# Prompt attention: the 128 x 128 turns of a block stand one by one between TensorE's other matmuls

## The chip, the cores and the metric

The kernel runs on one core of one Trainium2 chip. The metric is the time of one execution on the device in microseconds (us), as the median of three. A core has five engines that run side by side: TensorE (PE; its matrix unit shows as PE and its weight loads as PEld), ScalarE (ACT), VectorE (DVE), GpSimd (POOL) and SyncE (SP), which issues most of the transfers.

## The reference

One inference step of a two-layer encoder: 2048 prompt frames and 128 sample frames of width 1024. A gated short convolution comes first, then keys and values, then stick-breaking attention with 16 heads of 64, each layer with its norms and output projection. The change lies in the attention over the prompt:

```
z = q @ k.T * scale
log_keep = where(kpos < qpos, log_sigmoid(-z), 0)
after    = reverse cumulative sum of log_keep over the keys, without the key itself
a        = where(kpos < qpos, exp(log_sigmoid(z) + after), 0)
o        = a @ v
```

## The kernel before

**Tiling.** `phase_attend` goes through 8 pairs of heads, so 16 heads. A head has 10 units, each of 512 queries by 512 keys; 4 of them lie on the diagonal. A unit has 4 pieces (128 queries by up to 512 keys) and 4 blocks (128 keys by up to 512 queries). In all there are 640 pieces and 640 blocks.

**A piece.** TensorE scores it with two matmuls (L1806, L1807: the high and the low part of the keys against the same stationary queries). ScalarE takes two sigmoids of the score (L1882, L1883), VectorE runs the scan (L1933, L1939), GpSimd multiplies (L1989). The weights `a` now stand with queries on the partitions.

**A block.** The product with `v` needs keys on the partitions, so TensorE turns the block: `turn` (L1824 to L1834) issues one transposing matmul of 128 x 128 for each of its query tiles (L1832). That is four, or 4 - j for block j of a unit on the diagonal: 2176 turns in all. In a turn the stationary operand is the tile of `a` and the identity streams through. The turns of a block write one slot of `a_pt` (TS = 3 slots), and the last of them gives the semaphore `t_ready`. ScalarE copies the slot to `a_ath` (L1892, "high"), VectorE subtracts to get `a_atl` (L1949, "low"), and TensorE multiplies both with the values (L1819, L1821, "product").

**Chunks.** Between these TensorE also makes the projections of later heads' queries and of the gates: 280 chunks of six matmuls, 448 or 416 columns wide (L1850 to L1852).

**The order.** Every engine works through a list that `Line.draw_up` writes when the kernel is built. It plays the phase through with costs for each item (`work`, L1409 to L1439: the time that the engine is held, and the further time until the result is seen by others), and takes at each step the item that can start first, by `RANK` where several can. TensorE's list has the items score, turn, product and chunk. A turn costs `TURN * w / P` there, with 0.2 us more until it is seen (L1424). Chunks are let in by `spent`, the share of the planned time that is behind (L1457 to L1462). On the chip each engine then keeps its list's order and waits on semaphores.

Of the kernel before, what the change touches and what calls it, by code (L numbers as in the profile page):

```python
# [13 lines left out]
P = 128  # L14
# [15 lines left out]
QG = 4  # L30
# [1217 lines left out]

ENGINES = "PE", "ACT", "DVE", "POOL", "SP"
N_HEAD, N_OUT = 2 * NPAIR, 2 * NPAIR * NGQ  # L1250
TURN = 0.068
SCORE_LEAD, CHUNKS_END, CHUNKS_FROM, CHUNK_PACE = 13, 0.96, -0.01, 6


# [26 lines left out]
class Line:  # L1281


    def __init__(self):
        self.at = {}
        self.free = dict.fromkeys(ENGINES, 0.0)
        self.lines = {e: [] for e in ENGINES}
        self.loads = []
        self.pieces = [(h, n) for h in range(N_HEAD) for n in range(N_PIECE)]
        self.blocks = [(h, b) for h in range(N_HEAD) for b in range(N_BLOCK)]  # L1290
        self.outs = [(h, b) for h, b in self.blocks if ends_group(b)]
        self.chunks = all_chunks()
        self.gates = [c for c in self.chunks if c[3] == PARTS - 1]
        self.splits = [(un, m, half) for un in range(N_UN) for m in (Q, Z) for half in range(2) if (un, m) != (0, Q)]
        self.splits.sort(key=lambda s: (s[0], s[1]))
        self.next = collections.Counter()
        self.whole = sum(2 * pe_time(piece_width(n)) for _, n in self.pieces)
        self.whole += sum((QG - block_from(b) // P) * TURN + 2 * pe_time(QG * P - block_from(b))
                          for _, b in self.blocks)
        self.spent = 0.0  # L1300
        for part in range(PARTS):
            self.at["x", 0, 0, part] = X_LANDS[part]
        for half in range(2):
            self.at["split", 0, Q, half] = 0.0
        for h in range(2):
            for what in KEYS:
                self.at[what, h] = 0.0 if h == 0 else FIRST_DONE
            self.at["v_in", h] = V_LANDS if h == 0 else FIRST_DONE
        for m in (Q, Z):
            self.at["raw", 0, m] = 0.0  # L1310
        self.free["SP"], self.moved = X_LANDS[0] + 10.0, FIRST_DONE
# [97 lines left out]
    def work(self, what):  # L1409

        k = self.next[what]
        if what in ("score", "sigmoid", "scan", "weigh"):
            w = piece_width(self.pieces[k][1])
            if what == "score":
                return 2 * pe_time(w), 0.249 + 0.000469 * w - pe_time(w)
            if what == "sigmoid":
                return 2 * act_time(w), 0.185 - 0.000036 * w
            if what == "scan":
                return 0.06 + 0.0022 * w - (0.04 if w == P * QG and is_diagonal(PIECES[self.pieces[k][1]][0]) else 0), 0.135
            return pool_time(w), 0.09  # L1420
        if what in ("turn", "high", "low", "product"):
            w = QG * P - block_from(self.blocks[k][1])
            if what == "turn":
                return TURN * w / P, 0.2  # L1424
            if what == "high":
                return act_time(w), 0.185 - 0.000036 * w
            if what == "low":
                return dve_time(w), 0.15
            return 2 * pe_time(w), 0.249 + 0.000469 * w - pe_time(w)
        if what == "out":  # L1430
            return act_time(QG * P), 0.17
        if what == "values":
            return 1.12 + 2.4, 0.1
        if what == "split":
            return 1.21 + 0.69 + 1.24, 0.1
        w = PGROUPS[(self.chunks[k] if what == "chunk" else self.gates[k])[1]][1]
        if what == "chunk":
            return 3 * PART_KT * pe_time(w), 0.249 + 0.000469 * w - pe_time(w)
        return (act_time(w), 0.17) if what == "open" else (dve_time(w), 0.15)  # L1439
# [5 lines left out]
    def place(self, engine, what, start):  # L1445
# [12 lines left out]
        self.free[engine] = end = start + took  # L1458
        at = self.at
        line = self.lines[engine]  # L1460
        if engine == "PE" and what != "chunk":
            self.spent += took  # L1462
        end += seen
# [132 lines left out]
def phase_attend(nc, x_d, qz_v, w_room, qh_t, ql_t, kh_t, kl_t, sz_t, v_prompt, ident, oa_t, ob_t,  # L1596
# [4 lines left out]
    with ExitStack() as ctx:  # L1601
# [186 lines left out]
        def _(pe):  # L1788
            pe.sem_inc(t_ready, N_BLOCK)
            pe.sem_inc(av_done, N_BLOCK)  # L1790

            def score(pr, hh, n):
                u, q = PIECES[n]
                g, kp = UNITS[u]
                i, p0, w = QG * g + q, kp * Z_W, piece_width(n)
                if is_pair(pr, 0) and hh == 0:
                    if n == 0:
                        pe.wait_ge(early.first_loaded, 96)
                    elif g == ORDER[1] and is_diagonal(u) and q == 0:
                        pe.wait_ge(q_rest, 32)  # L1800
                elif n == 0:
                    pe.wait_ge(qk_loaded[hh], 96 * (pr + hh))
                pe.wait_ge(z_used, piece(pr, hh, n - ZS) + 1 + ZS)
                o = pz[:, n % ZS, 0:w]
                lhs = q2[hh][:, i * P:(i + 1) * P]
                pe.matmul(o, lhs, kh2[hh][:, p0:p0 + w], start=True, stop=False)  # L1806
                pe.matmul(o, lhs, kl2[hh][:, p0:p0 + w], start=False, stop=True).then_inc(z_ready, 1)  # L1807

            def multiply(pr, hh, b):
                u, j = BLOCKS[b]  # L1810
                c0, kb = block_from(b), QG * UNITS[u][1] + j
                first, last = is_diagonal(u) and j == 0, ends_group(b)
                if first:
                    wait_past(pe, o_read, (2 * pr + hh) * NGQ + ORDER.index(UNITS[u][0]))
                if b == 0:
                    pe.wait_ge(v_ready[hh], pr + 1)
                pe.wait_ge(at_split, blk(pr, hh, b) + 1)
                o = po[:, c0:QG * P]
                pe.matmul(o, v2[hh][:, kb, :, :], ath[:, b % AS, c0:], start=first, stop=False,  # L1819
                          skip_group_check=True)  # L1820
                pe.matmul(o, v2[hh][:, kb, :, :], atl[:, b % AS, c0:], start=False, stop=last,  # L1821
                          skip_group_check=True).then_inc(av_done, 1)

            def turn(pr, hh, b):  # L1824
                u, j = BLOCKS[b]
                if is_pair(pr, 0) and (hh, b) == (0, 0):
                    pe.wait_ge(ident_set, 1)
                if j == 0:
                    pe.wait_ge(weighted, piece(pr, hh, QG * u + QG) + N_PIECE)
                wait_past(pe, at_split, blk(pr, hh, b) + 1 - TS)  # L1830
                for q in range(block_from(b) // P, QG):
                    mm = pe.transpose(pt[:, turn_slot(pr, hh, b), q * P:(q + 1) * P].bitcast(F32R),  # L1832
                                      a_bits[:, unit_slot(hh, u), q, j * P:(j + 1) * P], ident_r[:, :])
                mm.then_inc(t_ready, 1)  # L1834

            def chunk(pr, gx, m, part):
                n = PGROUPS[gx][1]
                if part == 0:
                    if m == Z and makes_queries(pr, Q):
                        pe.wait_ge(q_low, NGX * pr + gx + 1)  # L1840
                    else:
                        wait_past(pe, z_gated, gate_number(pr, m, gx))
                if m == Q:
                    pe.wait_ge(x_loaded[part], 16 * (NGX * pr + gx + 1))
                if gx == 0 and part % (PARTS // 2) == 0:
                    pe.wait_ge(w_ready[m], 2 * pr + 1 + part // (PARTS // 2))
                for k in range(PART_KT):
                    kt = part * PART_KT + k
                    x_h, x_l = x[:, part, k, 0, 0:n], x[:, part, k, 1, 0:n]
                    pe.matmul(pq[:, 0:n], wh[m][:, kt, :], x_h, start=(kt == 0), stop=False)  # L1850
                    pe.matmul(pq[:, 0:n], wh[m][:, kt, :], x_l, start=False, stop=False)
                    mm = pe.matmul(pq[:, 0:n], wl[m][:, kt, :], x_h, start=False, stop=(kt == KT - 1))  # L1852
                if part == PARTS - 1:
                    mm.then_inc(pq_ready[m], 1)
                elif m == Z:
                    mm.then_inc(x_used[part], 1)

            def do(what, pr, hh, n):
                if what == "score":
                    score(pr, hh, n)  # L1860
                elif what == "turn":
                    turn(pr, hh, n)
                elif what == "product":
                    multiply(pr, hh, n)
                elif what == "chunk":
# [1 line left out]

            for item in lines["PE"]:
                do(*item)

        @block.scalar
        def _(act):
# [812 lines left out]
```

## Time and profile before

| | us |
|---|---|
| median of three runs (lowest, highest) | 2830.48 (2828.51, 2833.29) |
| the profiled execution | 2826.52 |
| its span, first to last instruction | 2824.9 |
| TensorE busy in it | 2767.3 |
| turns (L1832): 2176, first and last start | 1458.5, 2530.3 |

Times in the rows are us from the span's start. PE rows tell when a matmul starts and how long it is in the unit. Matmuls are pipelined, so what one costs is read from the starts of two that follow each other, not from its length. Several of one line in a row are merged ("x4"). A line of the program is written L1832. The granted clock is a share of 2.4 GHz.

### The profile page before, as it was taken

The page shows a single profiled execution, that of the slowest core. Times are in us where ns is not written, and L with a number is a line of the kernel's source. Part 1 is how long each engine was busy: PE and PEld are TensorE (multiplying, and loading weights), DVE is VectorE, ACT ScalarE, POOL GpSimd, SP SyncE. Part 2 cuts the span into 40 slices and gives each one's busy share as a digit, 9 for nine tenths or more (in the row PEclk, how much of TensorE's full clock was granted, in tenths as well). Part 3 has the DMA queues.
Part 4 walks back from the last instruction along what each step waited for, and adds up shares of the span by engine and source line. Part 5 has one row for each costly group of instructions (what it writes and reads, how often), then busy time and mean ns, then how long its engine had stood idle before and what let it go on. Part 6 is the DMA issues. An engine that isn't in the chain of part 4 may idle for free. (4 is left out here: it accounts for less than half of the span.)

```text
span 2824.9 us, 42046 instructions
## 1 busy us (share of the span) xinstructions
PE 2767.3 (98%) x14856; PEld 2420.5 (86%) x14856; DVE 1642.8 (58%) x2152; ACT 1316.6 (47%) x2733; POOL 1157.2 (41%) x1023
## 2 busy tenths in 40 slices
PE   7999999999999999999989999999999999989998
PEld 6999999999988888889978888888888888868886
DVE  5321232123244450102249999999999999998775
ACT  6000000000033341111148888888888888875443
POOL 3333333333220020002356877777777768651110
PEclk9999999999999999999999999999999999999999
DMA  5101110111064444424578676777777876767773
GB/s 159 39 25 37 38 38 22 38 38 38 9 210 134 126 155 151 173 102 153 166 216 267 197 244 198 236 215 216 221 223 208 251 203 208 220 187 210 231 225 105
DMA packets 280359, 433.33 MB, mean 153 GB/s; under 512 B 52578, under 2 KB 218594, under 8 KB 274180
## 3 DMA queue, kind: packets, MB, share of 16 engines
q1 hardware_dynamic: 269156, 391.41, 45.5%
q0 software_dynamic: 11040, 39.86, 4.8%
q8 instruction: 89, 1.46, 0.2%
q14 instruction: 74, 0.61, 0.1%
HBM read 307.40 MB, written 123.81 MB: 153 GB/s over the span
## 5 line engine op out<-in xcount | busy, mean ns | idle before, releaser
L1989 POOL TENSOR_TENSOR a_a<-a_a,a_prod 128x512 f32<-128x512 f32 (+3 forms) x640 | 661.9, 1052 | 272.0 <-DVE a_prod L1939 196.6
L1939 DVE TENSOR_TENSOR_SCAN a_prod<-a_keep,a_prod,a_restart 128x513 f32<-128x513 f32 x384 | 478.2, 1269 | 8.3 <-ACT a_keep L1883 7.5
L1882 ACT ACTIVATE a_a<-a_pz 128x512 f32<-128x512 f32 (+3 forms) x640 | 357.2, 559 | 70.9 <-PE a_pz L1807 46.6
L1949 DVE TENSOR_TENSOR a_atl<-a_pt,a_ath 128x512 fp32r<-128x512 f32 (+3 forms) x640 | 363.1, 599 | 32.3 <-ACT a_ath L1892 29.0
L1883 ACT ACTIVATE a_keep<-a_pz 128x512 f32<-128x512 f32 (+3 forms) x640 | 361.1, 565 | 0.0
L1892 ACT ACTIVATE a_ath<-a_pt 128x512 fp32r<-128x512 f32 (+3 forms) x640 | 332.8, 558 | 57.5 <-PE a_po L1821 34.1
L1832 PEld LDWEIGHTS a_pt<-a_ident,a_bits 128*128 128x128 f32 x2176 | 232.2, 141 | 51.7 <-DVE a_atl L1949 8.1
L279 POOL TENSOR_TENSOR w_wh<-w_raw,w_gain 128x1024 fp32r<-128x1024 f32 x22 | 42.6, 1936 | 534.6 <-PE v_pg L349 279.9
L1806 PE MATMUL a_pz<-a_kh,a_q 128*128 128x512 f32 (+3 forms) x640 | 247.6, 390 | 8.4 <-ACT a_keep L1883 5.8
L1819 PE MATMUL a_po<-a_ath,a_v 128*128 128x512 f32 (+3 forms) x640 | 250.1, 395 | 2.3 <-POOL a_v L2000 1.5
L1832 PE MATMUL a_pt<-a_ident,a_bits 128*128 128x128 f32 x2176 | 244.8, 242 | 7.1 <-DVE a_atl L1949 4.7
L1807 PE MATMUL a_pz<-a_kl,a_q 128*128 128x512 f32 (+3 forms) x640 | 234.0, 368 | 0.0
L347 PE MATMUL c_pg<-a_xh,w_wh 128*128 128x384 f32 (+1 forms) x640 | 231.1, 361 | 0.1
L347 PE MATMUL c_pg<-a_xh,c_wh 128*128 128x384 f32 (+1 forms) x640 | 230.7, 360 | 0.3 <-ACT c_cgate L496 0.3
L348 PE MATMUL c_pg<-a_xl,c_wh 128*128 128x384 f32 (+1 forms) x640 | 230.5, 360 | 0.0
L349 PE MATMUL c_pg<-a_xh,c_wl 128*128 128x384 f32 (+1 forms) x640 | 230.4, 360 | 0.0
L348 PE MATMUL c_pg<-a_xl,w_wh 128*128 128x384 f32 (+1 forms) x640 | 230.3, 360 | 0.0
L1821 PE MATMUL a_po<-a_atl,a_v 128*128 128x512 f32 (+3 forms) x640 | 229.1, 367 | 0.0
L349 PE MATMUL c_pg<-a_xh,w_wl 128*128 128x384 f32 (+1 forms) x640 | 228.8, 357 | 0.0
L531 DVE TENSOR_TENSOR c_u<-c_pg,c_cgate 128x512 f32<-128x512 f32 (+2 forms) x40 | 23.4, 586 | 317.9 <-PE c_pg L349 317.9
L1933 DVE TENSOR_TENSOR_SCAN a_prod<-a_keep,a_restart 128x128 f32<-128x128 f32 (+3 forms) x256 | 197.2, 805 | 8.7 <-ACT a_keep L1883 7.8
L500 ACT ACTIVATE c_sz<-c_pg 128x384 f32<-128x384 f32 (+1 forms) x40 | 21.4, 536 | 355.8 <-PE c_pg L349 355.8
(234 smaller groups left out, 6151.5 us busy)
## 6 DMA issues: line engine op xcount, KB each, us to landing
a_x<-x_d SPq DMA_DIRECT2D x84, 896.0 KB, 6.7
a_x<-x_d SPq DMA_DIRECT2D x56, 832.0 KB, 6.0
a_kh<-kh_t SPq DMA_DIRECT2D x32, 512.0 KB, 7.1
a_kl<-kl_t SPq DMA_DIRECT2D x32, 512.0 KB, 9.1
w_raw<-in_a_w_in POOLq DMA_DIRECT2D x30, 512.0 KB, 4.9
x<-f_xn POOLq DMA_DIRECT2D x17, 512.0 KB, 6.4
g_y_in<-sz_t SPq DMA_DIRECT2D x17, 512.0 KB, 7.6
g_x<-x SPq DMA_DIRECT2D x17, 512.0 KB, 4.1
```

The lines of the kernel that those rows point to most:

```text
L347: pe.matmul(out, w_h[:, kt, :], x_h[:, kt, r], start=(kt == 0), stop=False)
L348: pe.matmul(out, w_h[:, kt, :], x_l[:, kt, r], start=False, stop=False)
L349: mm = pe.matmul(out, w_l[:, kt, :], x_h[:, kt, r], start=False, stop=(kt == KT - 1))
L1806: pe.matmul(o, lhs, kh2[hh][:, p0:p0 + w], start=True, stop=False)
L1819: pe.matmul(o, v2[hh][:, kb, :, :], ath[:, b % AS, c0:], start=first, stop=False, skip_group_check=True)
L1832: mm = pe.transpose(pt[:, turn_slot(pr, hh, b), q * P:(q + 1) * P].bitcast(F32R), a_bits[:, unit_slot(hh, u), q, j * P:(j + 1) * P], ident ...
L1882: act.activation(a[:, s, q, 0:w], pz[:, n % ZS, 0:w], ACT.Sigmoid, scale=SCALE)
L1883: act.activation(keep[:, n % KS, 0:w], pz[:, n % ZS, 0:w], ACT.Sigmoid, scale=-SCALE).then_inc(z_used, 1)
L1892: act.activation(ath[:, b % AS, c0:], pt[:, turn_slot(pr, hh, b), c0:], ACT.Copy).then_inc(at_hi, 1)
L1939: dve.tensor_tensor_scan(prod[:, s, 0:w + 1][:, ::-1], keep[:, n % KS, 0:w + 1][:, ::-1], restart[:, 0:1].broadcast_to([P, w + 1]), prod[: ...
L1949: dve.tensor_tensor(atl[:, b % AS, c0:], pt[:, turn_slot(pr, hh, b), c0:], ath[:, b % AS, c0:].bitcast(F32), ALU.subtract).then_inc(at_spl ...
L1989: pool.tensor_tensor(part, part, prod[:, n % PS, after:after + w], ALU.mult).then_inc(weighted, 1)
```

## The change

Each block's turns go into a queue, `turns_left`. `turn` issues the first of them at once. After each following matmul of a score, a product or a chunk, `between` issues one more. `turn_rest` issues what is left before the next block's first turn, at a "rest" mark, and at the end of the list. The planner has a turn cost 0.0595 us in place of 0.068, has a block seen 0.21 us later for each turn past the first, and puts a "rest" mark ahead of an item that starts, in the plan, after the block's turns are to be seen.

```
-TURN = 0.068
+TURN, TURN_APART = 0.0595, 0.21
...
             if what == "turn":
-                return TURN * w / P, 0.2
+                return TURN * w / P, 0.2 + TURN_APART * (w // P - 1)
...
+        if engine == "PE":
+            if what != "turn" and start > self.turn_seen:
+                line.append(("rest", 0, 0, 0))
+            elif what == "turn":
+                self.turn_seen = end + seen
...
                 pe.matmul(o, lhs, kh2[hh][:, p0:p0 + w], start=True, stop=False)
+                between()
                 pe.matmul(o, lhs, kl2[hh][:, p0:p0 + w], start=False, stop=True).then_inc(z_ready, 1)
+                between()
...
-                for q in range(block_from(b) // P, QG):
-                    mm = pe.transpose(pt[:, turn_slot(pr, hh, b), q * P:(q + 1) * P].bitcast(F32R),
-                                      a_bits[:, unit_slot(hh, u), q, j * P:(j + 1) * P], ident_r[:, :])
-                mm.then_inc(t_ready, 1)
+                turns_left.extend((pr, hh, b, q) for q in range(block_from(b) // P, QG))
+                turn_one()
+
+            def turn_one():
+                pr, hh, b, q = turns_left.popleft()
+                u, j = BLOCKS[b]
+                mm = pe.transpose(pt[:, turn_slot(pr, hh, b), q * P:(q + 1) * P].bitcast(F32R),
+                                  a_bits[:, unit_slot(hh, u), q, j * P:(j + 1) * P], ident_r[:, :])
+                if q == QG - 1:
+                    mm.then_inc(t_ready, 1)
+
+            def turn_rest():
+                while turns_left:
+                    turn_one()
+
+            def between():
+                if turns_left:
+                    turn_one()
...
                 elif what == "turn":
+                    turn_rest()
                     turn(pr, hh, n)
+                elif what == "rest":
+                    turn_rest()
...
             for item in lines["PE"]:
                 do(*item)
+            turn_rest()
```

The products' two matmuls and the chunks' six have `between` after each of them in the same way.

## Rows read from the trace of the kernel before

**Rows 1.** The page: each engine's busy time, its share and its instructions.
```profile
PE 2767.3 (98%) x14856; PEld 2420.5 (86%) x14856; DVE 1642.8 (58%) x2152; ACT 1316.6 (47%) x2733; POOL 1157.2 (41%) x1023
```
**Rows 2.** Stretches of the span: window, length, busy time (instructions) by engine, clock, DMA.
```profile
core 0: us, PE busy (x) PEld busy (x) DVE busy (x) ACT busy (x) POOL busy (x), PEclk, DMA share, GB/s
1458.00:1560.00 102.00, 95.31 (x560) 81.75 (x560) 88.60 (x114) 80.49 (x177) 67.43 (x63) 1.00 0.87 251
1560.00:2440.00 880.00, 876.79 (x5323) 775.11 (x5322) 841.96 (x1112) 760.76 (x1691) 659.67 (x626) 1.00 0.74 220
2440.00:2535.00 95.00, 85.75 (x523) 73.57 (x522) 87.19 (x121) 77.92 (x176) 55.35 (x55) 0.96 0.62 187
```
**Rows 3.** TensorE in order of time around four turns in a row (start, duration).
```profile
1799.81 0.39 PE L1807 MATMUL a_pz<-a_kl,a_q 128*128 128x512 f32 x1
1800.04 0.46 PE L1832 MATMUL a_pt<-a_ident,a_bits 128*128 128x128 f32 x4
1800.34 0.46 PE L1806 MATMUL a_pz<-a_kh,a_q 128*128 128x512 f32 x1
1800.64 0.39 PE L1807 MATMUL a_pz<-a_kl,a_q 128*128 128x512 f32 x1
```
**Rows 4.** TensorE in order of time around twelve turns in a row.
```profile
2421.10 1.14 PE L1832 MATMUL a_pt<-a_ident,a_bits 128*128 128x128 f32 x12
2422.07 0.44 PE L1850 MATMUL a_pq<-a_x,a_wh 128*128 128x448 f32 x1
2422.34 0.37 PE L1851 MATMUL a_pq<-a_x,a_wh 128*128 128x448 f32 x1
2422.55 0.37 PE L1852 MATMUL a_pq<-a_x,a_wl 128*128 128x448 f32 x1
```
**Rows 5.** TensorE in order of time around a lone turn.
```profile
1802.77 0.39 PE L1821 MATMUL a_po<-a_atl,a_v 128*128 128x512 f32 x1
1803.00 0.22 PE L1832 MATMUL a_pt<-a_ident,a_bits 128*128 128x128 f32 x1
1803.06 0.45 PE L1806 MATMUL a_pz<-a_kh,a_q 128*128 128x512 f32 x1
1803.34 0.39 PE L1807 MATMUL a_pz<-a_kl,a_q 128*128 128x512 f32 x1
1803.57 0.40 PE L1806 MATMUL a_pz<-a_kh,a_q 128*128 128x512 f32 x1
```
**Rows 6.** The weight loads around the same lone turn.
```profile
1802.77 0.14 PEld L1832 LDWEIGHTS a_pt<-a_ident,a_bits 128*128 128x128 f32 x1
1803.00 0.19 PEld L1806 LDWEIGHTS a_pz<-a_kh,a_q 128*128 128x128 f32 x1
1803.11 0.19 PEld L1807 LDWEIGHTS a_pz<-a_kl,a_q 128*128 128x128 f32 x1
1803.34 0.19 PEld L1806 LDWEIGHTS a_pz<-a_kh,a_q 128*128 128x128 f32 x1
```
**Rows 7.** An early lone turn, and the last one, in order of time.
```profile
1499.63 0.22 PE L1832 MATMUL a_pt<-a_ident,a_bits 128*128 128x128 f32 x1
1499.69 0.39 PE L1806 MATMUL a_pz<-a_kh,a_q 128*128 128x384 f32 x1
1499.92 0.34 PE L1807 MATMUL a_pz<-a_kl,a_q 128*128 128x384 f32 x1
...
2530.28 0.22 PE L1832 MATMUL a_pt<-a_ident,a_bits 128*128 128x128 f32 x1
```
**Rows 8.** Line L1832 from 1458 to 2535 us: matmuls, min/median/max ns, first and last start.
```profile
L1832 PE MATMUL a_pt<-a_ident,a_bits x2176: 218/248/369, 1458.5 to 2530.3; 128*128 128x128 f32 x198
```
**Rows 9.** Who waited for whom from 1560 to 2440 us: total us, times, longest.
```profile
ACT a_ath L1892 <- PE a_po L1821: 27.3, 51, 2.0
DVE a_atl L1949 <- ACT a_ath L1892: 20.1, 56, 0.9
ACT a_ath L1892 <- PE a_pt L1832: 12.6, 24, 1.4
PE a_pz L1806 <- ACT a_keep L1883: 2.1, 3, 1.1
PEld a_pt L1832 <- DVE a_atl L1949: 1.9, 4, 1.2
```

More of the change, by code:

```diff
@@ L1299, in __init__ @@
                           for _, b in self.blocks)
-        self.spent = 0.0
+        self.spent, self.turn_seen = 0.0, 0.0
         for part in range(PARTS):
@@ L1790, in _ @@
             pe.sem_inc(av_done, N_BLOCK)
+            turns_left = collections.deque()
             def score(pr, hh, n):
@@ L1820, in multiply @@
                           skip_group_check=True)
+                between()
                 pe.matmul(o, v2[hh][:, kb, :, :], atl[:, b % AS, c0:], start=False, stop=last,
                           skip_group_check=True).then_inc(av_done, 1)
+                between()
             def turn(pr, hh, b):
@@ L1850, in chunk @@
                     pe.matmul(pq[:, 0:n], wh[m][:, kt, :], x_h, start=(kt == 0), stop=False)
+                    between()
                     pe.matmul(pq[:, 0:n], wh[m][:, kt, :], x_l, start=False, stop=False)
+                    between()
                     mm = pe.matmul(pq[:, 0:n], wl[m][:, kt, :], x_h, start=False, stop=(kt == KT - 1))
+                    if k < PART_KT - 1:
+                        between()
                 if part == PARTS - 1:
@@ L1856, in chunk @@
                     mm.then_inc(x_used[part], 1)
+                between()
             def do(what, pr, hh, n):
```

## The prediction

> **What bounds the kernel now.** I began with each engine's busy time: TensorE is busy for 98% of the span, and no other engine for more than 58% [rows 1]. The turns lie in the attention alone, 2176 of them from 1458.5 to 2530.3 us [rows 8], so I asked for the busy time by stretch there. In the 880 us from 1560 to 2440 TensorE is busy for 876.8, at the full clock (1.00, so 2.4 GHz), VectorE for 842.0, ScalarE for 760.8 [rows 2]. The first 102 us and the last 95 are looser, with TensorE idle for 6.7 and 9.3. Who waits for whom says the same: in the 880 us the longest waits of TensorE itself add up to 2.1 and 1.9 us [rows 9]. So the stage goes at the pace at which TensorE gets through its list. VectorE is a close second with 38 us of slack (880 less 842). What the change does to the time is, first, what it does to the number of nanoseconds that a turn takes from TensorE.
>
> A busy unit says nothing of that, because matmuls overlap; I therefore read starts in order of time. A matmul of 512 columns with no turn near starts its successor 0.23 us later (1803.34 to 1803.57 [rows 5]).
>
> **What a turn costs, in a row and alone.** Four in a row: from the first turn's start to the start of the second matmul behind them is 1800.64 - 1800.04 = 0.60 us [rows 3]. The wide matmul in between is worth 0.23, so the four cost 0.37. Twelve in a row: 2422.34 - 2421.10 = 1.24 [rows 4], less 0.21 for the 448 columns (2422.55 - 2422.34), so 1.03. The eight further turns cost 0.66, or 0.083 each; over all runs of 4 and of 12 with no wait I read 85 ns, which I use. A lone turn: 1803.34 - 1803.00 = 0.34 [rows 5], less 0.23, so 0.11. With three more at 0.085 this gives the 0.37 of the row of four. So n turns in a row cost 0.085 (n - 1) + 0.11.
>
> The point on which all hangs is how to read the lone turn. The next matmul starts only 0.06 us after it, which invites the thought that a turn standing alone costs 0.06. But that next matmul then lasts 0.05 longer than its kind (0.28 to its successor instead of 0.23). The loads say why [rows 6]: each begins when the matmul before has started, not earlier. The load for L1806 begins with the turn at 1803.00, and the next load can begin only 0.11 later, at 1803.11; a wide matmul hides such a load and a turn doesn't. A turn is a short matmul whose cost is the load behind it: 0.11 where that is an ordinary one, 0.085 where it is another turn's. There are 57 such lone turns (1458 to 2535 us, one undisturbed early one and the last in [rows 7]); the early one gives 1499.92 - 1499.63 = 0.29 for turn and 384 columns, which are worth 0.175 (384 / 512 of 0.23), so 0.11 again. The undisturbed ones all lie within some 5 ns of 0.11.
>
> **The change, part by part.** *Turns taken apart.* No turn is added or removed. What changes is how many are followed by an ordinary load. In the time-ordered rows I counted 464 runs of turns: 57 of one, 44 of two, 23 of three, 208 of four, 10 of five, 29 of seven, 54 of eight, 9 of nine, 29 of twelve, one of sixteen (2176 together). Now 464 turns have an ordinary load behind them and 1712 have a turn's. With the change a block that directly precedes another block's turns is still flushed in a row, since `turn` begins with `turn_rest`; only the last block of each run is spread. Of its m turns, m - 1 move, but no more are set apart than there are matmuls to follow: where only two matmuls stand before the next run, which is so behind 113 of the runs, only one is. Run by run, with min(m - 1, matmuls behind - 1), this comes to 220 blocks of four with room for all (660), 75 with room for one (75), 36 and 12 of three (72 + 12), 60 of two (60): 879 turns that go from 0.085 to 0.11. 879 x 0.0255 = **+22.4 us**, if the list keeps its order. The bounds: none set apart, 0; every inner turn, 1712 x 0.0255 = +43.7.
>
> *A load hidden better ahead of a turn.* A turn's own load now begins under a wide matmul. The first turn of a row has that already, and the others' load is the 0.085 that I count; what is hidden on one side is the 0.11 that appears on the other. Nothing further. Below it, the bound is the 0.06 of [rows 5], priced as a rival.
>
> *The block's result comes later.* In a row the last of four turns starts 3 x 0.085 = 0.26 us after the first. Apart, it starts after three turns and three wide matmuls, 3 x (0.11 + 0.23) = 1.02: 0.77 later. Behind it stand the copy L1892 on ScalarE and what follows it in ScalarE's list, then L1949 on VectorE, then the product and the turns three blocks on. The plan allows for 0.63 of it (3 x 0.21), and the list places products by that, so mostly it meets no one. Before, ScalarE waited for the turns 24 times, 12.6 us in all, and VectorE for that copy 56 times, 20.1 us [rows 9], and of both TensorE felt 1.9 us at L1832. If every one of the 24 waits grew by 0.77 and reached TensorE, that would be +18; over the whole stage, by TensorE's share, some 22. The other bound is below nothing: TensorE becoming slower by 2% gives the others time, and its remaining idle (3.2 us of 880, and 16 at both ends [rows 2]) could shrink, by 5 at the most. I take 0, as the row of what TensorE itself waits for is nearest to that.
>
> *Turns queued behind a wait.* A left-over turn can stand behind a score that waits for L1883, or a chunk that waits for its transfer. Those waits of TensorE are 2.1 us in three cases in the 880 us [rows 9], so below 3 us and within the bounds above.
>
> *The planner's costs.* It now believes that a turn takes 0.0595 where the rows show 0.085 to 0.11, so it plans a TensorE that is 18.5 us faster over the stage than in the old plan (2176 x 0.0085), while by my count it becomes 22 slower. The new list will have products and turns a little early against the other engines, but a TensorE that is slower than planned arrives later, not earlier, at each wait. SP's transfers and the chunks' pace go by shares of the plan and hardly move. A redrawn list can gain or lose a few us at the two loose ends: plus or minus 6.
>
> **The sum.** 2826.5 (profiled) + 22.4 + 0 + 0 = 2848.9. The profiled run was 4.0 under the median of the three, so 2852.9: I forecast **2853 us**, 22 slower (0.8%).
>
> **A rule against the trace.** The Trainium skill, "TensorE: Matmul & The Clock Gate", section "LDWEIGHTS (loading the stationary operand)", gives a load as its columns divided by 1.2, so 107 ns for 128, whatever is loaded. The ordinary loads agree (0.11 [rows 6]). By the rule alone a turn in a row would cost 0.107 as well, the 25 ns of difference would not exist and the sum would be nothing; the rows of four and of twelve, at 0.085, speak against it, and the measurement decides. This is rival B. The same page, section "Step-by-step: what each phase is for", has loads pulled ahead of in-flight matmuls. If several could be pulled ahead, a turn between two wide matmuls would cost its columns alone; this is rival A. The trace shows one load ahead and no more.
>
> **The rivals.** *A: turns apart are cheap* (the other side). Place: the 1343 turns (464 + 879) with an ordinary load behind. If in the alternating stream the load behind a turn were hidden too, each would cost the 0.06 between the starts of [rows 5]. Now the turns take 1712 x 0.085 + 464 x 0.11 = 196.6 us; then 833 x 0.085 + 1343 x 0.06 = 151.4: -45, so **2785 us**. It decides from 0.094 us per turn apart downwards ((196.6 - 70.8) / 1343). For it: the 0.06. Against it: the longer matmul behind, in all of the undisturbed lone turns.
>
> *B: no difference between apart and in a row*, or one that the new list gives back at the ends (up to 11 by the last bounds) and in the few runs that the new list packs more densely. **2830 to 2836 us**. For it: 25 ns is small, and the count of 879 rests on the old order. Against it: the rows of four and twelve.
>
> *C: the delay is felt.* VectorE has just 38 us of slack, and each block's copy comes up to 0.77 later. If these waits reach TensorE, the +18 to +22 come on top: **2875 us**, and up to 2895 with all 1712 turns apart.
>
> **Chances and range.** My forecast (2838 to 2868) 0.70; A 0.12; B 0.08; C 0.10. What the median of this kernel can tell from no change is about 0.2%, 5.7 us. Faster by more than that takes A and a sliver: 0.13. Within it B: 0.09. Slower: 0.78. The range has to leave out no more than 2 in 10: it runs from 2828, which takes in B and leaves out A, to 2882, which takes in most of C.
>
> **What would show it.** In the changed kernel the rows should have about 1340 runs of turns instead of 464, most of one turn; from a turn's start to the second start behind it still 0.34 us with 512 columns, now with a turn as that second start. The attention should be 22 us longer and all before the first turn (1458.5 us) the same; the waits of ScalarE for L1832 should be more, those of TensorE still a few us. I am wrong if that 0.34 is 0.29 (A), if the runs are many fewer than 1340 (the rest marks flush the blocks), or if TensorE's waits in the 880 us exceed some 10 us (C).

## The result, and the profile after

The changed kernel takes 2861.4 us (median, 2858.5 to 2862.5) against 2830.9 for the kernel before, measured side by side: 30.5 us slower, a ratio of 1.0109 with a 95% interval from 1.0094 to 1.0124. The forecast was 2853, in a range from 2828 to 2882.

The page, each engine's busy time, to be read against [rows 1]:

```profile
PE 2798.3 (98%) x14856; PEld 2430.9 (85%) x14856; DVE 1647.8 (58%) x2152; ACT 1322.2 (46%) x2733; POOL 1156.3 (40%) x1023
```

The number of instructions is the same on every engine. TensorE is busy for 31 us longer, no other engine for more than 6. TensorE's first score of the attention starts at 1453.2 us (1448.3 before) and its last product at 2566.9 (2532.3 before); a line of the program, with its count, min/median/max ns, first and last start:

```profile
L1812 PE MATMUL a_pz<-a_kh,a_q x640: 218/394/796, 1453.2 to 2553.1; 128*128 128x512 f32 x96, 128*128 128x128 f32 x64
L1830 PE MATMUL a_po<-a_atl,a_v x640: 271/396/735, 1485.7 to 2566.9; 128*128 128x512 f32 x160
```

So the attention is 1113.7 us long instead of 1084.1: 29.6 more. The 4.9 us by which it starts later are no effect of the change: in the ten profiles taken with the same work in the attention (the two kernels and eight of the experiments), all with the same code up to there, it starts between 1448.3 and 1454.2, and the kernel before happens to have the earliest start.

TensorE in order of time in the changed kernel (start, duration):

```profile
2105.82 0.22 PE L1847 MATMUL a_pt<-a_ident,a_bits 128*128 128x128 f32 x1
2105.88 0.45 PE L1827 MATMUL a_po<-a_ath,a_v 128*128 128x512 f32 x1
2106.17 0.22 PE L1847 MATMUL a_pt<-a_ident,a_bits 128*128 128x128 f32 x1
2106.23 0.45 PE L1830 MATMUL a_po<-a_atl,a_v 128*128 128x512 f32 x1
2106.52 0.37 PE L1847 MATMUL a_pt<-a_ident,a_bits 128*128 128x128 f32 x3
2106.73 0.47 PE L1812 MATMUL a_pz<-a_kh,a_q 128*128 128x512 f32 x1
2107.04 0.22 PE L1847 MATMUL a_pt<-a_ident,a_bits 128*128 128x128 f32 x1
```

From a lone turn to the next turn, with 512 columns between, is 0.35 us (2105.82, 2106.17, 2106.52). A wide matmul is worth 0.23, so the turn costs 0.12 at this resolution; the median of all 532 such places is 113 ns. The "x3" is two left-over turns and the first of the next block. There are 1330 runs of turns in place of 464, 1115 of them of one turn. The weight loads of the same stretch:

```profile
2105.82 0.19 PEld L1827 LDWEIGHTS a_po<-a_ath,a_v 128*128 128x128 f32 x1
2105.96 0.14 PEld L1847 LDWEIGHTS a_pt<-a_ident,a_bits 128*128 128x128 f32 x1
2106.17 0.19 PEld L1830 LDWEIGHTS a_po<-a_atl,a_v 128*128 128x128 f32 x1
```

A turn's own load (2105.96) now runs under the wide matmul that started at 2105.88, and the load of the matmul behind a turn (2105.82, 2106.17) begins only with the turn. Who waited for whom from 1565 to 2445 us (us, times, longest), against [rows 9]:

```profile
DVE a_atl L1982 <- ACT a_ath L1925: 45.0, 97, 1.0
ACT a_ath L1925 <- PE a_pt L1847: 43.4, 73, 2.0
ACT a_a L1915 <- PE a_pz L1814: 35.6, 64, 2.0
ACT a_ath L1925 <- PE a_po L1830: 18.9, 46, 1.1
PEld a_pz L1812 <- ACT a_keep L1916: 8.5, 22, 1.0
```

ScalarE now waits for turns 73 times and 43 us, where it was 24 times and 12.6 us, and VectorE waits twice as long for ScalarE's copy (45.0 us instead of 20.1). Part of the first is a change of name: ahead of the same copy the idle time put down to a product fell from 27.3 to 18.9, so all in all ScalarE's idle time there rose from 39.9 to 62.3 us. The last line has a counterpart in the kernel before that [rows 9] don't show:

```profile
PEld a_pz L1806 <- ACT a_keep L1883: 6.7, 17, 1.3
```

So the longest wait of TensorE's own in the middle was the score's for ScalarE's sigmoid L1883 (6.7 us at the weight load, 2.1 at the matmul), and it grew to 8.5. The busy time by stretch (length, then PE, PEld, DVE, ACT, POOL, clock), against [rows 2]:

```profile
1463.00:1565.00 102.00, 95.84 (x554) 81.51 (x553) 87.56 (x113) 79.95 (x176) 66.19 (x62) 1.00 0.87 250
1565.00:2475.00 910.00, 904.90 (x5360) 786.44 (x5360) 849.62 (x1121) 770.76 (x1701) 663.31 (x631) 1.00 0.72 213
2475.00:2570.00 95.00, 84.72 (x486) 70.18 (x485) 82.70 (x113) 74.19 (x165) 51.72 (x51) 0.95 0.60 184
```

TensorE's idle time in the middle is 5.1 us of 910 where it was 3.2 of 880. It is the bound as before, at the full clock in the middle; it has more to do.

**How I split the 29.6 us.** I gave each matmul of the attention its undisturbed step (start to start): 232, 202, 190, 175, 118 and 110 ns for 512, 448, 416, 384, 256 and 128 columns, a turn 110 where another matmul follows and 84.6 where a turn does. What of the phase's length this sum leaves over I call the remainder: waits, and late starts that no wait shows. Before: 1046.0 and a remainder of 38.1. After: 1068.0 and 45.7. So **22.0 us are turns** that have an ordinary load behind them now (866 more), and **7.6 us are remainder**. All kernels with the same work differ in this sum only by the number of their runs of turns, 25.4 ns each; that the sum agrees with a count of runs is therefore no further evidence, only the step itself is measured. Two limits: the undisturbed lone turns of the changed kernel lie up to 3 ns above the 110 that I gave them, so some 2 us of the 7.6 may be turns as well (an estimate from their starts); and a remainder comes from a single profile, so that a difference of 2 or 3 us between two of them says little.

### The profile page after: what moved, and what is told of

Same layout as the page of the kernel before. It is cut to its first block and busy times, and to the rows that moved or that the text cites. A ratio compares the mean times of both kernels' runs of the same rounds, so it can differ in the third digit from the quotient of the medians.

```text
span 2860.4 us, 42046 instructions
## 1 busy us (share of the span) xinstructions
PE 2798.3 (98%) x14856; PEld 2430.9 (85%) x14856; DVE 1647.8 (58%) x2152; ACT 1322.2 (46%) x2733; POOL 1156.3 (40%) x1023
## 5 line engine op out<-in xcount | busy, mean ns | idle before, releaser
L1982 DVE TENSOR_TENSOR a_atl<-a_pt,a_ath 128x512 fp32r<-128x512 f32 (+3 forms) x640 | 366.1, 600 | 65.2 <-ACT a_ath L1925 61.5
L1847 PE MATMUL a_pt<-a_ident,a_bits 128*128 128x128 f32 x2176 | 365.4, 233 | 4.5 <-DVE a_atl L1982 2.7
L1847 PEld LDWEIGHTS a_pt<-a_ident,a_bits 128*128 128x128 f32 x2176 | 271.0, 141 | 31.4 <-DVE a_atl L1982 5.0
L1812 PE MATMUL a_pz<-a_kh,a_q 128*128 128x512 f32 (+3 forms) x640 | 251.3, 394 | 12.2 <-ACT a_keep L1916 9.4
L1830 PE MATMUL a_po<-a_atl,a_v 128*128 128x512 f32 (+3 forms) x640 | 247.0, 394 | 0.0
L1814 PE MATMUL a_pz<-a_kl,a_q 128*128 128x512 f32 (+3 forms) x640 | 245.3, 384 | 0.0
```

The source lines that it names most:

```text
L1982: dve.tensor_tensor(atl[:, b % AS, c0:], pt[:, turn_slot(pr, hh, b), c0:], ath[:, b % AS, c0:].bitcast(F32), ALU.subtract).then_inc(at_spl ...
```

## The experiments

Two theories were to be tested. M: a short matmul costs the load behind it, 0.11 us for an ordinary one, 0.085 for a turn's. D: the rest of the loss is idle time because the turns' results come later.

**Turns in a row, in the changed kernel's list.** This undoes the spreading and keeps the redrawn list.

```
                 turns_left.extend((pr, hh, b, q) for q in range(block_from(b) // P, QG))
-                turn_one()
+                turn_rest()
```

> The changed kernel's list, with each block's turns in a row again (451 runs of turns, 1725 turns with a turn behind them). Theory M, a turn costs 0.11 us with an ordinary load behind it and 0.085 with a turn's: the turns cost 0.3 us less than in the kernel before, 22.4 less than in the changed one. Theory D, the some 8 us of further idle time of TensorE come from the later results of the turns: they go too. Together: 2831, between 2826 and 2836. Rival L, the idle time came with the redrawn list: it stays, 2838. Rival A is ruled out by the result already.

Measured: 2832.2 us, 1.0008 of the kernel before (0.9999 to 1.0017). The attention is 1084.9 us long, 1045.6 by steps and 39.3 of remainder. The list alone costs 2 us, with an interval that takes in nothing; the rest of the loss comes with the spreading. Rival L, by which 8 us stay with the redrawn list, is wrong.

**A row as late as the last turn.** The turns stand together, but only where the changed kernel would have the last of them.

```
-            turns_left = collections.deque()
+            turns_left, to_go = collections.deque(), [0]
...
                 turns_left.extend((pr, hh, b, q) for q in range(block_from(b) // P, QG))
-                turn_one()
+                to_go[0] = len(turns_left) - 1
+                if to_go[0] == 0:
+                    turn_rest()
...
             def between():
-                if turns_left:
-                    turn_one()
+                to_go[0] -= 1
+                if turns_left and to_go[0] <= 0:
+                    turn_rest()
```

> The changed kernel's list; a block's turns stand in a row, but where the changed kernel has the last of them, so the result is as late (578 runs of turns). Theory M: the turns cost 2.9 us more than before (114 x 0.0255). Theory D: the idle time of the changed kernel stays, some 8 us. Together 2841, between 2836 and 2847. Rival P, all of the 30 us comes from the later results and the neighbours don't matter: 2861. If D is wrong: 2834.

Measured: 2846.1 us, 1.0061 (1.0047 to 1.0074). TensorE in order of time:

```profile
1801.09 0.39 PE L1827 MATMUL a_po<-a_ath,a_v 128*128 128x512 f32 x1
1801.32 0.45 PE L1849 MATMUL a_pt<-a_ident,a_bits 128*128 128x128 f32 x4
1801.61 0.47 PE L1830 MATMUL a_po<-a_atl,a_v 128*128 128x512 f32 x1
1801.91 0.40 PE L1827 MATMUL a_po<-a_ath,a_v 128*128 128x512 f32 x1
```

1801.91 - 1801.32 = 0.59 for four turns and 512 columns: as in [rows 3], 0.36 for the four. The attention is 1098.8 us, 1048.9 by steps (578 runs) and 49.9 of remainder. So lateness, with the turns hardly dearer, brings 11.8 us of remainder, more than the 8 expected, and P (lateness is all) is wrong by 15 us. Its waits from 1565 to 2445 us show the first part of the path:

```profile
DVE a_atl L1985 <- ACT a_ath L1928: 38.4, 91, 1.0
ACT a_ath L1928 <- PE a_pt L1849: 37.4, 64, 1.9
```

and with the rows at once, in the run before this one:

```profile
DVE a_atl L1982 <- ACT a_ath L1925: 32.4, 71, 1.0
ACT a_ath L1925 <- PE a_pt L1847: 16.5, 26, 1.6
```

ScalarE's waits for turns more than double with the lateness; with those put down to products (L1830, 31.8 us before and 20.3 now) its idle time ahead of the copy rises from 48.3 to 57.7 us. Where TensorE feels it can be read over the whole attention (1448 to 2575 us). It is not at the turns: their matmuls' wait for VectorE's subtraction (L1949, L1982 in the changed kernel) is 4.7 us before and 2.7 in the changed kernel. It is the score's wait for ScalarE's second sigmoid:

```profile
PE a_pz L1806 <- ACT a_keep L1883: 5.8, 10, 1.2
PE a_pz L1812 <- ACT a_keep L1916: 9.4, 16, 1.4
PE a_pz L1812 <- ACT a_keep L1919: 11.8, 22, 1.6
```

These are the kernel before, the changed one and this one; with the rows at once it is 7.5 us in 12 times. ScalarE keeps its list's order, so a sigmoid behind a copy that waits is late too; that reading is mine and no run separates it. Nor do these waits make up the whole remainder. Why it is 4 us larger here than in the changed kernel I did not settle. TensorE has 19 us less to do here, so the others have less time; and TensorE's loader is idle ahead of L1812 for 9.6 us (24 times) that nothing in the profile ends, against 2.6 in the changed kernel. No run shows that either is the reason.

**Two turns at a time.**

```
                 turns_left.extend((pr, hh, b, q) for q in range(block_from(b) // P, QG))
-                turn_one()
+                between()
...
             def between():
-                if turns_left:
-                    turn_one()
+                for _ in range(2):
+                    if turns_left:
+                        turn_one()
```

> The changed kernel's list with two turns at a time between the matmuls (787 runs of turns). M: 323 more than the 464 before, x 0.0255 = 8.2 us. D: the last turn comes about half as late, so 2 to 6 us of idle time. Together 2843, between 2839 and 2847. Rival P (lateness alone): 2846 or more, with TensorE's own work unchanged. Rival Q, it is the number of alternations and each costs more than 0.0255 with others around: in proportion to the changed kernel's whole loss, 323/866 of 30 = 11, 2842, which the time can't tell from M and D, but the starts in the trace can.

Measured: 2843.5 us, 1.0051 (1.0037 to 1.0065), so 10.5 to 18.4 us more. By the trace 1054.2 by steps (787 runs), remainder 40.1. The turns' part is 8.2 by the count, and 553 rows of two take 196 ns in the median, 85 and 111, so an alternation costs no more here than elsewhere (rival Q asked for that). The remainder is 2.0 above the kernel before in this one profile, but the medians, 13.6 us apart, leave 5.4 beside the turns (2 to 10 by the interval). So whether half the lateness costs half or less is not shown.

**The old list, with the turns apart.** The costs of the plan are the old ones; only the rest marks allow for the spreading.

```
-TURN, TURN_APART = 0.0595, 0.21
+TURN, TURN_APART = 0.068, 0.21
...
-                return TURN * w / P, 0.2 + TURN_APART * (w // P - 1)
+                return TURN * w / P, 0.2
...
-                self.turn_seen = end + seen
+                k_w = (QG * P - block_from(self.blocks[k][1])) // P
+                self.turn_seen = end + seen + TURN_APART * (k_w - 1)
```

> The list of the kernel before (its costs and order unchanged), with the turns set one by one; the marks for the rest allow 0.21 us for each turn past the first, though the list doesn't (1341 runs of turns). M: 877 x 0.0255 = 22.4 us more than before. D: products and copies stand in their lists earlier than the turns now come, so more idle time than in the changed kernel, 8 to 20 us: 2861 to 2873, most likely 2865. Rival L (the redrawn list brought the idle time): 22 more and no idle time, 2853.

Measured: 2867.9 us, 1.0139 (1.0124 to 1.0155): 38 us. 1068.2 by steps (1341 runs), remainder 54.7. The turns cost 22.3 us by the count of runs, and the remainder is 16.6 above the kernel before. So the redrawn list is no cause of the loss; it spares 9 us of it by the traces, 7 by the medians.

**One more short plain matmul, with an ordinary load behind it.** In the kernel before:

```
+                pe.matmul(o[:, 0:64], lhs, kh2[hh][:, p0:p0 + 64], start=True, stop=True)
                 pe.matmul(o, lhs, kh2[hh][:, p0:p0 + w], start=True, stop=False)
```

> The kernel before, with one more matmul of 64 columns ahead of each score's first (640 in all, overwritten at once; the score is unchanged). Its columns are half of a turn's, the load behind it is an ordinary one. Theory M, the cost of a short matmul is the load behind it: 640 x 0.11 = 70 us, less 1 to 5 of idle time that it fills: 2898. Rival A', the cost is its columns (64 are 0.03 us with what stands around): 640 x 0.03 = 19, 2850. Rival R, a turn apart is dear because of the change between turning and plain matmuls: a plain matmul then costs its columns too, 2850.

Measured: 2894.7 us, 1.0230 (1.0214 to 1.0246): 65.5 us for 640. TensorE, and its loads, around one:

```profile
1942.84 0.19 PE L1806 MATMUL a_pz<-a_kh,a_q 128*128 128x64 f32 x1
1942.87 0.47 PE L1807 MATMUL a_pz<-a_kh,a_q 128*128 128x512 f32 x1
1943.18 0.39 PE L1808 MATMUL a_pz<-a_kl,a_q 128*128 128x512 f32 x1
```

```profile
1942.84 0.19 PEld L1807 LDWEIGHTS a_pz<-a_kh,a_q 128*128 128x128 f32 x1
1942.95 0.19 PEld L1808 LDWEIGHTS a_pz<-a_kl,a_q 128*128 128x128 f32 x1
```

The next matmul starts 0.03 us behind it, and the one after at 1943.18: 0.34 in all, less 0.23 is 0.11. Half of a turn's columns, no turning, and the same price as a lone turn. It is the load behind. The attention grows by 66.1 us, 70.4 by count; 4 us of idle time were filled.

**One more short plain matmul, ahead of turns.**

```
+                q = QG - 1
+                pe.matmul(pt[:, turn_slot(pr, hh, b), q * P:q * P + 64],
+                          ident_r[:, :], ident_r[:, 0:64], start=True, stop=True)
                 for q in range(block_from(b) // P, QG):
```

> The kernel before, with one more plain matmul of 64 columns ahead of each block's first turn (640 in all, overwritten by the turns). The load behind it is a turn's. Theory M, what counts is which load comes behind: 640 x 0.085 = 54 us, less 1 to 5 of idle time: 2882. Rival K, what counts is the matmul's own kind, so a plain one costs 0.11 wherever it stands: 70 us, 2898. In a run of several blocks the extra matmul's own ordinary load stands behind another turn (176 places, 0.0255 each, 4.5 us more by M): 2886.

Measured: 2891.8 us, 1.0220 (1.0204 to 1.0235): 62.6 us. At the head of a run, the loads:

```profile
1828.17 0.40 PEld L1835 LDWEIGHTS a_pt<-a_ident,a_bits 128*128 128x128 f32 x4
1828.51 0.19 PEld L1806 LDWEIGHTS a_pz<-a_kh,a_q 128*128 128x128 f32 x1
1828.62 0.19 PEld L1807 LDWEIGHTS a_pz<-a_kl,a_q 128*128 128x128 f32 x1
```

and the matmuls:

```profile
1828.16 0.19 PE L1832 MATMUL a_pt<-a_ident 128*128 128x64 f32 x1
1828.19 0.52 PE L1835 MATMUL a_pt<-a_ident,a_bits 128*128 128x128 f32 x4
1828.55 0.46 PE L1806 MATMUL a_pz<-a_kh,a_q 128*128 128x512 f32 x1
1828.85 0.39 PE L1807 MATMUL a_pz<-a_kl,a_q 128*128 128x512 f32 x1
```

1828.85 - 1828.16 = 0.69 for the extra, four turns and 512 columns, where [rows 3] has 0.60: 0.09 for the extra. The first turn's load begins as the extra starts, at 1828.17, and from there the four turns' loads take (1828.51 - 1828.17) / 4 = 0.085 each, the first one like the others, where the ordinary one behind them takes 0.11. The median over the 464 such places is 85 ns. The same short plain matmul ahead of a score cost 0.11, so its own kind is not what counts (K is wrong). Within a run of turns (176 places) the extra costs 0.131, not 0.11:

```profile
1873.97 0.19 PEld L1832 LDWEIGHTS a_pt<-a_ident 128*128 128x128 f32 x1
1874.11 0.40 PEld L1835 LDWEIGHTS a_pt<-a_ident,a_bits 128*128 128x128 f32 x4
```

Its load begins at 1873.97 and the turn's 0.13 to 0.14 later. 464 x 0.085 + 176 x 0.131 = 62.5, against 62.6 measured; the interval is 58 to 66, so the match to 0.1 is luck, but K's 70.4 lies outside it. The time alone lay 6 to 10 us above what I expected by M and 6 below K; why an ordinary load between two turns' takes 0.02 more than next to ordinary ones stays open.

**True costs in the plan, turns in a row.** The kernel before with `TURN = 0.0915`.

```
-TURN = 0.068
+TURN = 0.0915
```

> The kernel before, with the planner's cost of a turn set to what the traces show in a row, on average 0.0915 us in place of 0.068 (466 runs of turns). M: the turns cost the same. If the plan's error cost idle time, up to the 12 us of TensorE's lost time in the stage's middle could come back: 2822. If the list's order is tolerant, as theory D has it (only results later than planned cost): 2831, within 4.

Measured: 2825.1 us, 0.9985 (0.9976 to 0.9994). A part came back: the remainder fell from 38.1 to 32.6 us at the same sum of steps (1046.0, 466 runs). This is faster than the kernel before by 0.15%: just clear of no difference by its interval, though below the 0.2% that I had set myself.

**True costs in the plan, turns apart.**

```
-TURN, TURN_APART = 0.0595, 0.21
+TURN, TURN_APART = 0.103, 0.26
```

> The changed kernel, with the planner's costs set to what its trace shows: 0.103 us for a turn on average and 0.26 for each further turn of a block (1438 runs of turns, 108 more than in the changed one). M: 2.8 us more than the changed kernel. D: the idle time that came with the change, some 8 us, goes in good part because the plan now knows how late the turns come: 2856 to 2862, most likely 2858. If D is wrong: 2864.

Measured: 2862.3 us, 1.0114 (1.0098 to 1.0129). 1070.7 by steps (1438 runs, 2.8 more by their count), and a remainder of 46.7. My guess that the remainder would go was wrong: this plan, with the costs that the trace shows, doesn't get rid of what the lateness costs. The score's wait for the sigmoid is only 5.3 us here, so that wait alone is not the remainder.

**Fewer, longer runs.** Two versions of the kernel before with the plan's costs by M, to see whether the opposite of the change pays. The second alone has the condition with `needs.append`; the rest is in both.

```
-TURN = 0.068
+TURN, RUN_END = 0.085, 0.0255
...
+                last = self.lines[engine]
+                after_turn = bool(last and last[-1][0] == "turn")
+                if not after_turn and k % 2 == 0 and k + 1 < len(self.blocks):
+                    needs.append(self.back("low", k + 1, TS))
-                yield "turn", self.when(*needs), RANK["turn"]
+                yield "turn", self.when(*needs), -1 if after_turn else RANK["turn"]
...
+        if engine == "PE" and what != "turn" and self.lines[engine] and self.lines[engine][-1][0] == "turn":
+            took += RUN_END
```

> The kernel before with a planner that knows what M says: 0.085 us for a turn, 0.0255 more for the first other matmul behind turns; and a turn that can start right behind another is taken first (401 runs of turns instead of 464). M: 63 x 0.0255 = 1.6 us less for the turns. The truer costs: as in the run with 0.0915, some 4 us less idle time. Together 5 to 6 us under the kernel before: 2824. If an order with turns first makes scores and products late (theory D on the other items): 2828 to 2832.

> As run_joined, but an even-numbered block's turns also wait in the plan until the next block's slot is free, so two blocks stand in one row (301 runs of turns). M: 163 x 0.0255 = 4.2 us less for the turns, plus the 4 of the truer costs: 2821 if nothing else happens. Theory D: every first block of two comes later, by up to the 1.7 us that a block takes, and idle time of TensorE rises by 5 to 20: 2828 to 2840. I hold the second for likelier.

Measured against 2829.9 us for the kernel before: 2828.1 us (0.9998, 0.9989 to 1.0007) without the condition, 2825.2 (0.9985, 0.9976 to 0.9994) with it. By steps 1044.4 (401 runs) and 1041.8 (301 runs), 1.6 and 4.2 less by the count; remainders 38.1 and 38.8. The time of the first is not clear of no difference. That of the second is, and its 4.2 us fit the count, but the truer costs alone had brought as much in the run with 0.0915, so the times don't show which of the two it was. By the remainders the gain of the truer plan was gone in both. The idle time that I held for likely with two blocks in a row did not come.

## Why the forecast was right, and where it was off

- *TensorE bounds the stage, so what a turn takes from it is what counts.* Right, and shown best by the two runs with extra matmuls: 70.4 and 62.5 us of steps were added, and the attention grew by 66.1 and 62.0. It is not all: with the same work in the attention the remainder still lies anywhere from 32.6 to 54.7 us in ten kernels, so it is no constant.
- *A lone turn costs 0.11, not the 0.06 to the next start.* Right, and the step on which the sign hung. In the changed kernel lone turns cost 111 to 114 ns in the median (by the width of the matmul behind, 256 to 512 columns), and a plain matmul with half the columns costs 0.11 as well, so it is the load behind and neither columns nor turning. Rival A would have needed 0.094 or less.
- *879 turns would be set apart.* There are 866 more runs: 22.0 us against the forecast's 22.4. The old list was a good enough basis for counting.
- *The rule against the trace.* The Trainium skill ("TensorE: Matmul & The Clock Gate", section "LDWEIGHTS (loading the stationary operand)") has 128 columns load in 107 ns. That fits an ordinary load (108 ns from load to load). For a turn's load it would give rival B; the trace gives 85, also where the matmul ahead of it is a plain one.
- *A load hidden better ahead of a turn gives nothing.* Right; nothing negative appears in the sum.
- *The later results cost 0.* This is the term that was mis-sized. I bounded it by -5 and +22 and took 0, because TensorE's own waits at L1832 were tiny. It measured +7.6 in the changed kernel's trace, 11.8 with the lateness alone, 16.6 where the list knew nothing of it. I had named a path (turn, L1892, L1949, the turns three blocks on) and then judged it by the wait at its far end, which didn't grow. I also read TensorE's longest waits as 2.1 and 1.9 us and passed over the 6.7 us of the score's load behind L1883; it is there that TensorE's waits grew, and so the copy's delay came in more by ScalarE's sigmoids than by VectorE. ScalarE's 24 waits for turns were a better sign: they became 73. With the 7.6, and the same 4 us between profile and median, the sum would have been 2860.5; 2861.4 was measured. The 4 us are the distance of one profiled run from its median, no effect, so that closeness is in part luck.
- *TensorE's waits in the 880 us stay a few us, and more than 10 would be C.* Its idle time in the middle is 5.1 us of 910, by busy time. C as a mechanism, lateness felt by TensorE, is real by the run with the late rows, at a third of the price that I gave it.
- *The phases ahead are the same.* The same code and work, but their length moves by some 5 us from run to run, so a single pair of profiles is to be compared phase by phase and not by its spans (35.5 apart, where the medians are 30.5 apart).

## What to carry to other kernels

Price a short matmul by the start of the second matmul behind it, not the first, and look at which load stands behind. Here a short one paid for the next weight load, so turns are cheaper together, where their own quick loads stand behind them; joining them beyond the order of the kernel before brought nothing that the times show for certain. Count the changes of neighbour in the order as it is; that count held within 2%. For a result that comes later, look at the first engine that waits for it and how often, and at what else that engine gives to the bound one. Don't put the loss at zero when the second engine is 96% busy, as here.

## What was not expected of the hardware

A turn's weight load occupies the loader for less time (85 ns from load to load, 141 ns as recorded) than an ordinary one of the same 128 x 128 (108 and 188 ns). After an ordinary load that itself follows a turn's, the next turn's load begins only 0.131 us later (176 places); the changed kernel has the same in 999 places, 132 ns in the median, but a wide matmul mostly covers it there. Why turns' loads are quicker, and why this step is longer, no run shows. And of the plan, not the hardware: a cost for a turn that was 26% too small cost 0.15% of the time (0.06 to 0.24 by the interval).
